# The last pair of experts in a two-layer transformer kernel: row products, gating and transposes in another order

## The chip, the cores and the metric

The kernel is one program on one NeuronCore of a Trainium2 chip. The metric is the device time of one launch in microseconds (us); of several runs the median is taken. The engines named here are TensorE (PE in the profile, its weight loads PEld), VectorE (DVE), ScalarE (ACT), GpSimd (POOL) and SyncE (SP), which in this kernel issues the loads from HBM. All data are 32-bit floats, and each matmul in the source leaves two records in the trace, so that "x16" in a row of PE is eight matmuls of the program (transposes written as such leave one record each).

## The reference, cut to what matters

Two networks of two layers each run one after the other on 256 tokens of width 1024. In the second network each layer ends with a mixture of 32 experts, of which each token uses two. The change touches this part alone:

```
def expert_block(args):
    xblk, e = args
    hid = jax.nn.silu(xblk @ w_gate[e]) * (xblk @ w_up[e])
    return hid @ w_down[e]

yb = lax.map(expert_block, (xb, block_e)).reshape(n_rows, d)
return jnp.zeros_like(h).at[row_tok].add(yb * row_w[:, None])
```

A router picks the experts and the weights `row_w`; `xb` holds the tokens' rows sorted by expert. An expert has 1024x512 gate and up weights and 512x1024 down weights. The weights of two experts are 12 MB, and all 16 pairs of a layer are read whatever the router says.

## The kernel before

`experts(l)` exists once for each engine and runs twice, for layer 0 (from about 824 us of the span) and layer 1 (from about 1385 us, up to the final norm). Each pair of experts i = 0..15 is worked on by hand-written code that is the same in shape for each i; each engine runs its own list in program order and waits on counters (semaphores) that the others raise.

**A pair on TensorE.** At most 64 tokens (`CAP`) go to an expert; two experts fill 128 rows of a product. `product_of(0, i, ...)` multiplies the gathered tokens `xg` with the gate weights into bank 0 of PSUM, `product_of(1, ...)` with the up weights into bank 1: eight steps k, each of two matmuls of 64 columns of tokens against 512 weights (`gate_step`, the rows of L1543), the two experts side by side in the array. Steps 0 to 3 use the first half of a weight matrix, 4 to 7 the second; `half_arrived` waits for its load. `turn_hidden` transposes the gated rows `hs` (128x512) in four 128x128 pieces back into bank 0 (L1642); `turn_weights` transposes the router's weights for the pair (L1630, bank 2); `scatter` adds the rows of the pair before, `yt`, to the tokens' sums in banks 4 to 7, in eight products m = 0..7 (`add_rows`, L1504), of which m = 0..3 read the first half of `yt` and m = 4..7 the second. I call one of these eight a row product. `down` multiplies the transposed hidden rows `hg` with the down weights, columns 0..511 (c = 0) into bank 0 and then 512..1023 (c = 1) into bank 1, k = 0..3 in each (L1673).

**A pair on the other engines.** ACT turns bank 0 into its sigmoid (`gate_sig`) and, after `down`, copies banks 0 and 1 into the halves of `yt` (`yt_ready`, twice a pair). DVE multiplies sigmoid and gate (L3375 in the last pair), multiplies with bank 1 into `hs` once up is full (L3378, raises `hid_ready`), copies the transposed rows to `hg` (L3380, raises `hg_ready`), and copies the transposed weights to `spread` (L3383, raises `spread_ready`).

**The loads.** SP issues the weights of pair i as their places in SBUF come free, that is, as PE finishes with what lay there. For the last pairs they come in halves of 2 MB, and the second half of the last pair's down weights in two parts of 1 MB (`load_last_half`, L1836).

**The last pair** (i = 15) is written out by itself. Its row products stand: three between the halves of gate (`first_rows`), three between the halves of up (`later_rows`), one after up, one after `turn_weights`. Before the first up product PE waits for `yt_ready` to reach twice the pair's number.

**The start of the stage.** `keep_clock(n)` multiplies zeros with zeros into unused banks, n products of 128x128 (L1444). It is called twice in `experts`: between the two products that count the chosen experts, and after these, once the token rows are there (`htok_ready`), ahead of `gather(e_, 0)`. `gather` picks the first pair's tokens by a product with the mask `pick` (L1497), which DVE makes at L3284 (`masks_ready`).

Of the kernel before, what the change touches and what calls it, by code (L numbers as in the profile page):

```python
# [17 lines left out]
ALU = mybir.AluOpType  # L18
# [3 lines left out]
P = 128  # L22
D = 1024
KT = D // P
# [11 lines left out]
HTL = HALF // P  # L36
# [24 lines left out]
EH = 512  # L61
# [104 lines left out]
def build(nc, a, out):  # L166
    with ExitStack() as ctx:
# [82 lines left out]
        ident = cst("ident")  # L250
# [361 lines left out]
        def _(pe):  # L612
# [810 lines left out]
            def experts(l):  # L1423
# [18 lines left out]
                def keep_clock(n):  # L1442
                    for i in range(n):
                        mm(ps[:, 4 + i % 4, 0:P], zeros[:, 0:P], zeros[:, 0:P], start=True, stop=True)  # L1444
# [17 lines left out]
                    open_bank(b)  # L1462
                    owner[b] = None
                turn.take(S["htok_ready"], 4)
                keep_clock(2)
                pe.wait_ge(e_["masks_ready"], 1)
                gather(e_, 0)
                gather(e_, 1)
# [131 lines left out]
            def gathered_tokens(e_, first):  # L1600
# [32 lines left out]
                def scatter(m0=0, m1=KT, begins=False):  # L1633
                    for m in range(m0, m1):
                        last = add_rows(m, begins=begins)
                    if m1 == KT:
                        last.then_inc(e_["scattered"], 1)

                def turn_hidden(i):
                    pe.wait_ge(e_["hid_ready"], i + 1)  # L1640
                    for m in range(HTL):
                        last = nc.tensor.transpose(ps[:, 0, m * P:(m + 1) * P], hs[:, m * P:(m + 1) * P], ident)  # L1642
                    last.then_inc(e_["hid_turned"], 1)
# [11 lines left out]
                        add_rows(m, of_first=True)  # L1655

                def down(i):
                    pe.wait_ge(e_["hg_ready"], i + 1)
                    for c in range(2):
                        in_two = c == 1 and isinstance(i, int) and i == last_pair  # L1660
                        if in_two:
                            first_part_arrived(first)
                        else:
                            half_arrived(first, 2, i, c)
                        for k in range(HTL):
                            if in_two and k == HTL // 2:
                                half_arrived(first, 2, i, c)
                            for e in range(2):
                                at = k * PAIR + e * CAP
                                tile, to = tile_of(first, 2, i, c, e, k), ps[e * CAP:(e + 1) * CAP, c, :]  # L1670
                                if places_of(2, i)[c] is None:
                                    to = to.rearrange("p (a b) -> p a b", a=4)
                                last = mm(to, hg[:, at:at + CAP], tile, start=(k == 0), stop=(k == HTL - 1))  # L1673
                        last.then_inc(e_["down_done" if c else "half_done"], 1)
# [38 lines left out]
                    scatter(0, 3)  # L1713

                def later_rows():
                    scatter(3, KT - 2)

                product_of(0, last_pair, 0, e_["gate_full"], first_rows)
                pe.wait_ge(e_["yt_ready"], 2 * last_pair)
                product_of(1, last_pair, 0, e_["up_full"], later_rows)  # L1720
                scatter(KT - 2, KT - 1)
                turn_hidden(last_pair)
                turn_weights(last_pair)
                scatter(KT - 1, KT)
                down(last_pair)

# [752 lines left out]
        def _(dve):  # L2479
# [851 lines left out]
            def gathered_tokens(e_):  # L3331

                def hidden_rows(i):
                    dve.wait_ge(e_["gate_sig"], i + 1)
                    V.tensor_tensor(eg, ps[:, 0, :], sg, ALU.mult).then_inc(e_["gated"], 1)  # L3335
                    dve.wait_ge(e_["gated"], i + 1)
                    dve.wait_ge(e_["up_full"], i + 1)
                    V.tensor_tensor(hs, ps[:, 1, :], eg, ALU.mult).then_inc(e_["hid_ready"], 1)  # L3338
                    dve.wait_ge(e_["weights_turned"], i + 1)

                def turned(i):
                    V.tensor_copy(spread, ps[:, 2, 0:T]).then_inc(e_["spread_ready"], 1)
                    dve.wait_ge(e_["hid_turned"], i + 1)
                    V.tensor_copy(hg, ps[:, 0, :]).then_inc(e_["hg_ready"], 1)

                last_pair = NEXP // 2 - 1
                for i in range(2):
                    dve.wait_ge(e_["gate_sig"], i + 1)
                    V.tensor_tensor(eg, ps[:, 0, :], sg, ALU.mult).then_inc(e_["gated"], 1)
                    dve.wait_ge(e_["weights_turned"], i + 1)  # L3350
                    V.tensor_copy(spread if i else first_spread, ps[:, 2, 0:T]).then_inc(e_["spread_ready"], 1)
                    masks(e_, i + 1)
                    dve.wait_ge(e_["gated"], i + 1)
                    dve.wait_ge(e_["up_full"], i + 1)
                    V.tensor_tensor(hs, ps[:, 1, :], eg, ALU.mult).then_inc(e_["hid_ready"], 1)
                    dve.wait_ge(e_["hid_turned"], i + 1)
                    V.tensor_copy(hg, ps[:, 0, :]).then_inc(e_["hg_ready"], 1)
                def middle_pair(i):
                    hidden_rows(i)
                    masks(e_, i + 1)  # L3360
                    if isinstance(i, int) and i < BLOCKS:
                        dve.wait_ge(e_["scattered"], i - 1)
                        turned(i)
                    else:
                        dve.wait_ge(e_["hid_turned"], i + 1)
                        V.tensor_copy(hg, ps[:, 0, :]).then_inc(e_["hg_ready"], 1)
                        dve.wait_ge(e_["scattered"], i - 1)
                        V.tensor_copy(spread, ps[:, 2, 0:T]).then_inc(e_["spread_ready"], 1)

                for i in range(2, BLOCKS + 1):  # L3370
                    middle_pair(i)
                with dve.Fori(0, last_pair - BLOCKS - 1) as n:
                    middle_pair(n + BLOCKS + 1)
                dve.wait_ge(e_["gate_sig"], last_pair + 1)
                V.tensor_tensor(eg, ps[:, 0, :], sg, ALU.mult).then_inc(e_["gated"], 1)  # L3375
                dve.wait_ge(e_["gated"], last_pair + 1)
                dve.wait_ge(e_["up_full"], last_pair + 1)
                V.tensor_tensor(hs, ps[:, 1, :], eg, ALU.mult).then_inc(e_["hid_ready"], 1)  # L3378
                dve.wait_ge(e_["hid_turned"], last_pair + 1)
                V.tensor_copy(hg, ps[:, 0, :]).then_inc(e_["hg_ready"], 1)  # L3380
                dve.wait_ge(e_["scattered"], last_pair - 1)
                dve.wait_ge(e_["weights_turned"], last_pair + 1)
                V.tensor_copy(spread, ps[:, 2, 0:T]).then_inc(e_["spread_ready"], 1)  # L3383
# [272 lines left out]
```

## Time and profile before

| | |
|---|---|
| median of 3 runs | 1843.9 us (1843.64 to 1845.76) |
| the profiled execution: its device time | 1845.65 us |
| its span, first to last instruction | 1843.8 us |
| TensorE busy | 1787.9 us, 97% of the span |
| VectorE, ScalarE busy | 781.4 us, 387.5 us |
| loads on the hardware queue | 589.63 MB |
| chain that ended last, by engine | PE 82%, DMA 14%, DVE 2%, ACT 1% |
| mean granted TensorE clock | 0.992 |

The times of the profile count from the span's start. A row of the timeline says when an instruction started, how long it took, its engine and line, output and input by name, and in brackets how long the engine had been idle before it and what ended that. Work that overlaps on one engine is pipelined: a matmul's record lasts longer than the time after which the next can start.

### The profile page before, as it was taken

What the parts mean: (1) busy time and instruction counts of PE and PEld (TensorE: products, weight loads), DVE (VectorE), ACT (ScalarE), POOL (GpSimd) and SP (SyncE); (2) the same over time, 40 slices, a digit from 0 to 9 for tenths busy, and PEclk for the clock granted to TensorE, in tenths of its full rate; (3) what the DMA queues carried; (4) which work ended last, traced back from release to release, by engine and by line L of the source; (5) the groups of instructions that cost most, each with busy time, mean ns of one, the idle gap of its engine ahead of it and who ended that gap; (6) DMA issues with size and microseconds to landing.
All of it is one profiled execution on the core that took longest, in us unless ns stands there. A gap on an engine that the chain in (4) does not pass through costs nothing.

```text
span 1843.8 us, 25756 instructions
## 1 busy us (share of the span) xinstructions
PE 1787.9 (97%) x10782; PEld 1197.4 (65%) x10786; DVE 781.4 (42%) x1501; ACT 387.5 (21%) x830; POOL 17.8 (1%) x31
## 2 busy tenths in 40 slices
PE   8999999999999999999999998899999999998998
PEld 7799999858999997674454343345985444443333
DVE  5978878873886964533111011014533111110112
ACT  3441110433311113522211111112113211110111
POOL 1000000000000100000000000000000000000000
PEclk9999999999999999999999999999999999999999
DMA  8664687725347764159999999999478999999996
GB/s 313 228 274 163 270 336 303 292 101 221 145 191 290 312 241 191 71 211 358 427 427 433 425 433 428 433 424 425 200 279 342 427 427 429 430 431 431 430 427 254
DMA packets 55406, 593.31 MB, mean 322 GB/s; under 512 B 6272, under 2 KB 18560, under 8 KB 22400
## 3 DMA queue, kind: packets, MB, share of 16 engines
q1 hardware_dynamic: 54720, 589.63, 77.7%
q10 hardware_dynamic: 576, 2.10, 0.3%
q8 instruction: 84, 1.38, 0.3%
q14 instruction: 26, 0.21, 0.0%
HBM read 588.91 MB, written 1.05 MB: 320 GB/s over the span
## 4 chain that ended last, share of the span: by engine, by line
PE 82%; DMA 14%; DVE 2%; ACT 1%; issue 1%; DVEq 0%; SPq 0%
PE ps L1543 19%; PE ps L883 14%; DMA ring<-in_w_up 13%; PE ps L670 13%; PE ps L1673 8%; PE ps L960 8%; PE ps L1504 4%; PE ps L1497 2%; PE ps L745 1%; PE ps L824 1%; PE ps L1079 1%; PE ps L1321 1%; PE ps L1281 1%; PE ps L1738 1%; PE ps L730 1%; PE ps L777 1%
## 5 line engine op out<-in xcount | busy, mean ns | idle before, releaser
L1543 PE MATMUL ps<-ring,work 128*64 128x512 f32 x1376 | 312.6, 609 | 29.8 <-DMA ring<-in_w_up 29.8
L1543 PEld LDWEIGHTS ps<-ring,work 128*64 128x64 f32 x1376 | 100.5, 140 | 232.7 <-issue 198.9
L2020 ACT ACTIVATE work<-ps 128x512 f32<-128x512 f32 (+1 forms) x168 | 89.8, 539 | 702.9 <-PE ps L1673 248.5
L1673 PE MATMUL ps<-ring,work 128*64 128x512 f32 x896 | 199.0, 595 | 0.3
L3335 DVE TENSOR_TENSOR work<-ps,work 128x512 f32<-128x512 f32 x26 | 18.0, 692 | 382.8 <-ACT work L2020 382.8
L670 PE MATMUL ps<-hsq,ring 128*128 128x256 f32 x768 | 169.9, 380 | 0.3 <-DVE hsq L2575 0.3
L670 PEld LDWEIGHTS ps<-hsq,ring 128*128 128x128 f32 x768 | 144.7, 190 | 22.8 <-issue 3.4
L1543 PE MATMUL ps<-spare,work 128*64 128x512 f32 x528 | 148.6, 592 | 0.0
L883 PE MATMUL ps<-hsq,ring 128*128 128x128 f32 x1280 | 147.2, 275 | 0.6 <-issue 0.5
L883 PEld LDWEIGHTS ps<-hsq,ring 128*128 128x128 f32 x1280 | 145.2, 192 | 1.9 <-issue 1.7
L1673 PEld LDWEIGHTS ps<-ring,work 128*64 128x64 f32 x896 | 62.0, 137 | 120.8 <-issue 119.1
L1504 PE MATMUL ps<-work 128*128 128x256 f32 x512 | 121.5, 381 | 0.0
L883 PE MATMUL ps<-hsq,spare 128*128 128x128 f32 x960 | 110.5, 275 | 0.0
L883 PEld LDWEIGHTS ps<-hsq,spare 128*128 128x128 f32 x960 | 109.0, 192 | 0.4
L1543 PEld LDWEIGHTS ps<-spare,work 128*64 128x64 f32 x528 | 47.1, 137 | 95.5 <-issue 95.5
L2496 DVE SCALAR_TENSOR_TENSOR work<-ring,silu_c,work 128x512 f32<-128x512 f32 x140 | 105.2, 752 | 4.8
L1504 PEld LDWEIGHTS ps<-work 128*128 128x128 f32 x512 | 92.6, 190 | 18.2 <-issue 8.1
L3338 DVE TENSOR_TENSOR work<-ps,work 128x512 f32<-128x512 f32 x26 | 18.0, 692 | 194.2 <-PE ps L1543 194.2
L2020 ACT ACTIVATE work<-hsq 128x512 f32 x60 | 38.1, 635 | 208.7 <-PE ps L1543 201.7
L670 PE MATMUL ps<-work,ring 128*128 128x256 f32 x352 | 79.1, 382 | 0.9 <-DVE work L3175 0.9
L670 PEld LDWEIGHTS ps<-work,ring 128*128 128x128 f32 x352 | 66.1, 190 | 13.8 <-issue 3.9
L1543 PE MATMUL ps<-work 128*64 128x512 f32 x144 | 64.8, 593 | 0.0
(386 smaller groups left out, 2019.1 us busy)
## 6 DMA issues: line engine op xcount, KB each, us to landing
ring<-in_w_up SPq DMA_DIRECT2D x30, 2048.0 KB, 13.3
ring<-in_w_up SPq DMA_DIRECT2D x14, 4096.0 KB, 21.7
ring<-in_w_down SPq DMA_DIRECT2D x14, 4096.0 KB, 20.5
ring<-in_w_ada SPq DMA_DIRECT2D x24, 2048.0 KB, 13.6
ring<-in_w_gate SPq DMA_DIRECT2D x24, 2048.0 KB, 12.9
ring<-in_w_down SPq DMA_DIRECT2D x24, 2048.0 KB, 16.3
spare<-in_w_gate SPq DMA_DIRECT2D x10, 3072.0 KB, 19.2
ring<-in_w_ff_gate SPq DMA_DIRECT2D x10, 2048.0 KB, 8.4
```

Of the source, the lines that this page charges most:

```text
L670: last = mm(ps[:, b, 0:T], w[:, k, m * P:(m + 1) * P], rhs[:, k, :], start=(i == 0), stop=(i == nk - 1))
L730: last = mm(ps[:, b, 0:P], w[:, k, m * P:(m + 1) * P], rhs[:, k, half(t)], start=(k == 0), stop=(k == KT - 1))
L745: last = mm(ps[:, banks[m], half(t)], w[:, k, m * P:(m + 1) * P], u[:, k, half(t)], start=(k == 0), stop=(k == KT - 1))
L777: last = mm(ps[QUAD * g:QUAD * g + QUAD, b, 0:T], taps_of(GROUPS * j + g), data_of(GROUPS * j + g), start=start, stop=stop)
L883: last = mm(ps[:, b, at:at + P], tile_of(w, k, m), rows[:, k, :], start=(begins and w == m == k == 0), stop=(k == HTL - 1), skip_group_che ...
L960: last = mm(ps[:, b, m * P:(m + 1) * P], tile_of(k, m), rows[:, k, :], start=(s == m == k == 0), stop=(k == nk - 1), skip_group_check=True)
L1497: last = mm(ps[:, 3 - half, k * PAIR:(k + 1) * PAIR], htok[:, t, (4 * half + k) * P:(4 * half + k + 1) * P], pick[:, t, :], start=(t == 0) ...
L1504: return mm(ps[:, 4 + m // 2, (m % 2) * T:(m % 2 + 1) * T], rows, first_spread if of_first else spread, start=begins and m % 2 == 0, stop= ...
L1543: last = mm(ps[e * CAP:(e + 1) * CAP, w, :], xg[:, k, e * CAP:(e + 1) * CAP], tile_of(first, w, i, 2 * k // KT, e, k % HTL), start=(k == 0 ...
L1673: last = mm(to, hg[:, at:at + CAP], tile, start=(k == 0), stop=(k == HTL - 1))
L2020: return nc.scalar.activation(out_, in_, f, bias=bias, scale=scale, **kw)
L2496: return V.scalar_tensor_tensor(out=out_, in0=in0, scalar=scalar, in1=in1, op0=op0, op1=op1)
```

## The change

Four things change, in both layers:

1. The second call of `keep_clock(2)` goes.
2. Row products 3 and 4 move from between the halves of up to ahead of up (behind the wait for `yt_ready`); row product 5 stays between the halves.
3. DVE makes `hs` in two instructions of 256 columns, each raising `hid_ready`. PE transposes columns 0..255 into bank 0, the weights next, then columns 256..511 into bank 3 (`turn_half`); DVE copies the two parts to `hg` by two instructions of 256 columns, each raising `hg_ready`.
4. `down` of the last pair begins once the first part of `hg` is there and waits for the second ahead of k = 2.

```
                 turn.take(S["htok_ready"], 4)
-                keep_clock(2)
                 pe.wait_ge(e_["masks_ready"], 1)
...
                 def down(i):
+                    of_last = isinstance(i, int) and i == last_pair
                     pe.wait_ge(e_["hg_ready"], i + 1)
...
                         for k in range(HTL):
+                            if of_last and c == 0 and k == HTL // 2:
+                                pe.wait_ge(e_["hg_ready"], last_pair + 2)
...
                 def later_rows():
-                    scatter(3, KT - 2)
+                    scatter(KT - 3, KT - 2)
+
+                def turn_half(part):
+                    pe.wait_ge(e_["hid_ready"], last_pair + 1 + part)
+                    for m in range(HTL // 2 * part, HTL // 2 * (part + 1)):
+                        last = nc.tensor.transpose(ps[:, 3 * part, m * P:(m + 1) * P], hs[:, m * P:(m + 1) * P], ident)
+                    last.then_inc(e_["hid_turned"], 1)
...
                 pe.wait_ge(e_["yt_ready"], 2 * last_pair)
+                scatter(3, KT - 3)
                 product_of(1, last_pair, 0, e_["up_full"], later_rows)
                 scatter(KT - 2, KT - 1)
-                turn_hidden(last_pair)
+                turn_half(0)
                 turn_weights(last_pair)
+                turn_half(1)
                 scatter(KT - 1, KT)
                 down(last_pair)
...
-                V.tensor_tensor(hs, ps[:, 1, :], eg, ALU.mult).then_inc(e_["hid_ready"], 1)
-                dve.wait_ge(e_["hid_turned"], last_pair + 1)
-                V.tensor_copy(hg, ps[:, 0, :]).then_inc(e_["hg_ready"], 1)
+                parts = [slice(p * EH // 2, (p + 1) * EH // 2) for p in range(2)]
+                for cols in parts:
+                    V.tensor_tensor(hs[:, cols], ps[:, 1, cols], eg[:, cols], ALU.mult).then_inc(e_["hid_ready"], 1)
+                for p, cols in enumerate(parts):
+                    dve.wait_ge(e_["hid_turned"], last_pair + 1 + p)
+                    V.tensor_copy(hg[:, cols], ps[:, 3 * p, cols]).then_inc(e_["hg_ready"], 1)
```

On TensorE, from the first up product of layer 1's last pair to the start of down, the program before has these rows (L1543 up, L1504 row products, L1642 and L1630 transposes, L1673 down; in brackets the counters waited for):

```order
L1543 MATMUL ps<-ring,work 64x512 [waits slot5_loaded,expert_yt_ready_1]
L1543 MATMUL ps<-ring,work 64x512 x7
L1504 MATMUL ps<-work 128x256 x3
L1543 MATMUL ps<-ring,work 64x512 [waits slot6_loaded]
L1543 MATMUL ps<-ring,work 64x512 x7
L1504 MATMUL ps<-work 128x256
L1642 MATMUL ps<-con,work 128x128 [waits expert_hid_ready_1]
L1642 MATMUL ps<-con,work 128x128 x3
L1630 MATMUL ps<-con,work 128x128 [waits expert_spread_ready_1,expert_masks_ready_1]
L1630 MATMUL ps<-con,work 128x128
L1504 MATMUL ps<-work 128x256
L1673 MATMUL ps<-ring,work 64x512 [waits slot0_loaded,expert_hg_ready_1]
```

The changed program has at the head of this stretch (its lines are numbered differently: L1542 up, L1503 row products):

```order
L1503 MATMUL ps<-work 128x256 [waits expert_yt_ready_1]
L1503 MATMUL ps<-work 128x256
L1542 MATMUL ps<-ring,work 64x512 [waits slot5_loaded]
L1542 MATMUL ps<-ring,work 64x512 x7
L1503 MATMUL ps<-work 128x256
L1542 MATMUL ps<-ring,work 64x512 [waits slot6_loaded]
```

Two row products stand ahead of up and one between its halves. At the end of the stretch, from the row product after up on, it has (L1723 transposes of the hidden rows, L1629 of the weights, L1675 down):

```order
L1503 MATMUL ps<-work 128x256
L1723 MATMUL ps<-con,work 128x128 [waits expert_hid_ready_1]
L1723 MATMUL ps<-con,work 128x128
L1629 MATMUL ps<-con,work 128x128 [waits expert_spread_ready_1,expert_masks_ready_1]
L1629 MATMUL ps<-con,work 128x128
L1723 MATMUL ps<-con,work 128x128 [waits expert_hid_ready_1]
L1723 MATMUL ps<-con,work 128x128
L1503 MATMUL ps<-work 128x256
L1675 MATMUL ps<-ring,work 64x512 [waits slot0_loaded,expert_hg_ready_1]
L1675 MATMUL ps<-ring,work 64x512 x3
L1675 MATMUL ps<-ring,work 64x512 [waits expert_hg_ready_1]
L1675 MATMUL ps<-ring,work 64x512 x3
```

The weights' transposes now stand between the two halves of the hidden rows' transposes, and down has one wait more.

On VectorE the last pair of layer 1 stands in the program before as:

```order
L3375 TENSOR_TENSOR work<-ps,work 128x512 [waits expert_gate_sig_1]
L3378 TENSOR_TENSOR work<-ps,work 128x512 [waits expert_up_full_1,expert_gated_1]
L3380 COPY work<-ps 128x512 [waits expert_hid_turned_1]
L3383 COPY work<-ps 128x256 [waits expert_weights_turned_1,expert_scattered_1]
L3402 UNCONDITIONAL_BRANCH
```

and in the changed one as:

```order
L3385 TENSOR_TENSOR work<-ps,work 128x512 [waits expert_gate_sig_1]
L3390 TENSOR_TENSOR work<-ps,work 128x256 [waits expert_up_full_1,expert_gated_1]
L3390 TENSOR_TENSOR work<-ps,work 128x256
L3393 COPY work<-ps 128x256 [waits expert_hid_turned_1] x2
L3396 COPY work<-ps 128x256 [waits expert_weights_turned_1,expert_scattered_1]
```

Two instructions of 512 columns have become four of 256.

## Rows read from the trace of the kernel before

**Rows 1.** The chain that ended last (start us, us, what), last two pairs.

```profile
1756.64 8.78 PE ps L1543 x32
...
1787.04 23.58 DMA ring<-in_w_up
```

**Rows 2.** Timeline, TensorE and VectorE, layer 1's last pair from the second half of gate.

```profile
1806.57 0.64 PE L1543 MATMUL ps<-spare,work 128*64 128x512 f32 x1
...
1810.76 3.65 PE L1543 MATMUL ps<-ring,work 128*64 128x512 f32 x16 [0.53 <-DMA ring<-in_w_up]
...
1814.35 1.56 PE L1504 MATMUL ps<-work 128*128 128x256 f32 x6
...
1815.84 3.65 PE L1543 MATMUL ps<-ring,work 128*64 128x512 f32 x16
...
1819.61 0.69 DVE L3378 TENSOR_TENSOR work<-ps,work 128x512 f32<-128x512 f32 x1 [8.01 <-PE ps L1543]
...
1820.36 0.66 PE L1642 MATMUL ps<-con,work 128*128 128x128 f32 x4 [0.23 <-DVE work L3378]
...
1821.05 0.69 DVE L3380 COPY work<-ps 128x512 f32<-128x512 f32 x1 [0.75 <-PE ps L1642]
1821.07 0.60 PE L1504 MATMUL ps<-work 128*128 128x256 f32 x2
1821.70 0.42 DVE L3383 COPY work<-ps 128x256 f32<-128x256 f32 x1
...
1821.80 7.09 PE L1673 MATMUL ps<-ring,work 128*64 128x512 f32 x32
```

**Rows 3.** Issues on SP for this pair's up weights, and the second one's time to landing.

```profile
1787.04 3.76 SPq L1815 DMA_DIRECT2D ring<-in_w_up  x2
...
ring<-in_w_up SPq DMA_DIRECT2D x1, 2048.0 KB, 25.0
```

**Rows 4.** The same for its down weights: three issues, their times to landing.

```profile
1798.33 0.33 SPq L1815 DMA_DIRECT2D ring<-in_w_down  x1
1801.76 0.90 SPq L1836 DMA_DIRECT2D ring<-in_w_down  x2
...
DMA to landing us min/median/max: 21.2/22.1/23.2
```

**Rows 5.** Timeline around the first gather, layer 1, then layer 0.

```profile
1390.72 0.43 DVE L3284 TENSOR_TENSOR work<-con,work 128x256 f32<-128x256 f32 x1
1391.09 0.69 PE L1444 MATMUL ps<-zeros 128*128 128x128 f32 x4
1391.62 3.74 PE L1497 MATMUL ps<-work 128*128 128x128 f32 x32
1393.60 1.51 ACT L2020 ACTIVATE work<-ps,ada,scale_g 128x128 f32<-128x128 f32 x4 [1.94 <-PE ps L1497]
...
829.63 0.42 DVE L3284 TENSOR_TENSOR work<-con,work 128x256 f32<-128x256 f32 x1
830.52 3.74 PE L1497 MATMUL ps<-work 128*128 128x128 f32 x32
```

**Rows 6.** Stretch: engines' busy time (instructions), granted clock, DMA share, GB/s; SP's issue.

```profile
1424.00:1426.00 2.00, 2.00 (x12) 0.61 (x10) 0.00 (x0) 0.00 (x0) 0.00 (x0) 1.00 0.81 229
...
1424.45 0.33 SPq L1810 DMA_DIRECT2D spare<-in_w_up  x1
```

**Rows 7.** Timeline from layer 0's last pair to the first products of layer 1's mixer.

```profile
1257.24 3.65 PE L1543 MATMUL ps<-ring,work 128*64 128x512 f32 x16
...
1281.64 1.23 DVE L2732 TENSOR_TENSOR spare<-ring 128x1024 f32<-128x1024 f32 x1 [1.27 <-DMA ring<-in_w_odd]
...
1285.03 3.31 ACT L2020 ACTIVATE hsq<-hsq,ada 128x256 f32<-128x256 f32 x8 [3.20 <-DVE hsq L3433]
...
1288.76 3.73 PE L883 MATMUL ps<-hsq,ring 128*128 128x128 f32 x32 [0.50 <-issue]
```

**Rows 8.** A stretch after a long wait of TensorE; columns as in Rows 6.

```profile
1756.00:1764.00 8.00, 7.36 (x28) 2.36 (x30) 0.00 (x0) 0.00 (x0) 0.00 (x0) 0.79 0.95 410
```

More of the change, by code:

```diff
@@ L1657, in down @@
                 def down(i):
+                    of_last = isinstance(i, int) and i == last_pair
                     pe.wait_ge(e_["hg_ready"], i + 1)
                     for c in range(2):
-                        in_two = c == 1 and isinstance(i, int) and i == last_pair
+                        in_two = c == 1 and of_last
                         if in_two:
```

## Prediction

> **What bounds the kernel now.** I read the chain that ended last first, then the timeline of each place that the diff names, and last the issues and landings of the loads there. In the last pairs of a layer the chain alternates between TensorE products and the loads of the up weights: 8.78 us of products in pair 13, and then, for pair 15, a load of up weights that ran 23.58 us from its issue at 1787.04 [rows 1]. It landed at 1810.62, and TensorE began the up products at 1810.76, 0.14 us later, after 0.53 us without work [rows 2]. From there to the end nothing is late but TensorE itself and the two hand-overs with VectorE between up and down: up's second half began at 1815.84, the gated rows were made from 1819.61 to 1820.30, turned from 1820.36, copied from 1821.05 to 1821.74, and down began at 1821.80 [rows 2]. That is 5.96 us from the start of up's second half to down. Down's own loads were not late: issued at 1798.33, 1801.76 and about 1802.2, with 22.1, 21.2 and 23.2 us to landing, they were there at 1820.4, 1823.0 and 1825.4 [rows 4].
>
> **Steps of TensorE that I use.** The 16 records of a half of gate or up take 3.59 us until a row product can start (1810.76 to 1814.35), and six records, three row products, take 1.49 us until the products of 64 columns go on (1814.35 to 1815.84) [rows 2]. At 0.43 us each, the rate at which eight pairs of side by side records fill 3.43 us of a half, three are 1.30 and the change back costs 0.19; the change into them costs 0.15. So one row product costs 0.43, and a group of them 0.34 more wherever it stands between such products.
>
> **Part 1, the zeros ahead of the first gather.** The zeros began at 1391.09 and the gather at 1391.62. What the gather needs besides is the mask, finished by VectorE at 1390.72 + 0.43 = 1391.15 [rows 5]. VectorE's hand-over to TensorE took 0.06 us at the turns [rows 2]; I allow up to 0.14, the delay seen behind a load. So the gather begins between 1391.21 and 1391.29, that is 0.33 to 0.41 us earlier; I take 0.35. ScalarE waited 1.94 us for the gather's first half and had nothing else to do, so it moves along [rows 5]. In layer 0 the mask ended at 830.05 and the gather began at 830.52, the same distance: 0.35 again. Does this reach the end, when later pairs wait for loads? The stream of loads is full only from a certain point on; in the stretch from 1424 the DMA share was still 0.81 with 229 GB/s, and the next issue, at 1424.45, waited for a product of TensorE [rows 6]. Everything behind that gap is issued and lands earlier by as much as TensorE is. So both the products and the stream shift by 0.35 in each layer.
>
> **Part 2, two row products ahead of up.** The second half of gate began at 1806.57 and would end, for a row product, at 1810.16. Two row products and the change back take 0.87 + 0.19 = 1.06: up can begin at 1811.21, 0.45 later than before. The load landed at 1810.62, so nothing is waited for. Up's first half, one row product and the change back take 3.59 + 0.43 + 0.19 = 4.21 (before 5.08), so TensorE would be ready for the second half at 1815.42, 0.42 earlier than 1815.84: the wait and its reaction (0.77 over the pure sequence) are filled, less 0.34 for one more group of row products. But now the second load counts. Its issue is the last 0.33 us of a row of two that ends at 1790.80, thus 1790.47, and it took 25.0 us: landed at 1815.47 [rows 3]. With the reaction of 0.14 the second half begins at 1815.61. The gain is 0.23 and not 0.42.
>
> **Part 3, hidden rows in two parts.** Counting from the start of up's second half: VectorE begins at +3.77. A PSUM instruction of 512 columns took 0.69 as product or as copy, a copy of 256 took 0.42 [rows 2]; no row here shows the product at 256, and between 0.35 (half of 0.69) and 0.42 I take the copy's 0.42, since product and copy agree at 512. First part ready +4.19, turned from +4.25. Six transposes fill the 0.71 us from 1820.36 to the row product at 1821.07, so one occupies TensorE for 0.12; the copy of four began 0.69 after their start, 0.22 behind the last one's slot [rows 2]. Two then take 0.24 and are seen at 0.46: the first copy runs from +4.71 to +5.13 and down could start at +5.19. TensorE meanwhile: weights' transposes to +4.73, the second half's to +4.97 (its rows were ready at about +4.6), the last row product with the change back 0.62, to +5.59. Down starts at +5.59, held by TensorE's own work, against +5.96: 0.37 gained, between 0.2 (if the second hand-over costs TensorE another 0.15) and 0.45. The second copy of `hg` ends near +5.6 and is needed at +5.59 + 1.72. At 1815.61 + 5.59 = 1821.20 the down weights of 1820.4 are there; the last of them, 1825.4, is wanted at 1826.4.
>
> The Trainium skill speaks against this part: VectorE: DVE Perf Modes, section on the TRN2 errata, says that each VectorE instruction pays a fixed latency and advises tiles of 512 elements or more. The trace agrees about the price: 0.69 and 0.42 leave a fixed part of 0.15, twice more here. By that rule alone the part would lose 0.30; it doesn't, as the second parts lie beside TensorE's row product.
>
> **Layer 0's last pair** would gain in the same way, and I book nothing for it. Its up half began at 1257.24; the pair ends some 13 us before the next mixer. There VectorE waited for a load of the odd layer's weights until 1281.64, with 1.27 us idle; behind that stand the reciprocal and the eight scalings, which feed ScalarE until 1288.34; and TensorE, idle for 0.50 us, began at 1288.76 [rows 7]. That load is in the full stream, which moves with part 1 and not with the last pair. What TensorE gains in the last pair it waits longer at 1288.76.
>
> **The sum.** 0.35 + 0.35 from the gathers, 0.23 + 0.37 from layer 1's last pair: 1.3 us. Against the profiled execution's 1845.65 (its span 1843.8 and 1.85 around it) that is 1844.35. This execution lies at the upper end of the three runs; on their median, 1843.9, it gives 1842.6, and that is the forecast.
>
> **Rivals.**
> (a) Layer 0's last pair counts after all, by 0.5 us: if TensorE and not ScalarE ends the 0.50 us of idle time at 1288.76. Against it stands that ScalarE's eighth row ends at 1288.34, later than the last product before. It would give 1842.1.
> (b) The stream of loads does not follow the gather, because its rate and not the gap of rows 6 decides when the late loads land. Then part 1 is swallowed in both layers, and 0.6 is left: 1843.3.
> (c) The last pair gives nothing: the load of up's second half lands a little later against TensorE than here, or the second hand-over in three steps costs what the first saves. Parts 2 and 3 cancel and part 1 stays: 1843.2.
> (d) Slower: the zeros kept TensorE's clock. After a wait of some 4 us the granted clock was 0.79 in a stretch of 8 us, partly at the lower level of 1.2 GHz [rows 8], and the up products took 8.78 us, where the 32 records of down took 7.09 at full clock: 1.7 us lost [rows 1, 2]. If each gather fell so, the loss is 3.4 against gains of 1.3: 2.1 slower, 1846.0. It decides once the two layers together lose 1.3 us, which is 2.6 us at half rate. A loss over 0.2% would need about 10 us at half rate. Against it: the zeros fill only 0.45 us and the mask's wait leaves at most 0.2 us idle in their place; the other call stays.
> The Trainium skill, TensorE: Matmul & The Clock Gate, Part 1, says that the gate goes by how busy the array has lately been; that is the ground of (d), and the stretch of rows 8, behind a wait, agrees.
> That the change doesn't do what it says is (c) in another form.
>
> **How the numbers follow.** A measurement of this kernel can tell about 0.2%, 3.7 us, from no change. Forecast 0.55, (a) 0.12, (b) 0.13, (c) 0.15, (d) 0.05. All but the far end of (d) lie within 0.2%. What can lead beyond is the spread of the runs: before's three span 2.1 us, so a median may lie 1.9 above or somewhat below. I give faster 0.03, within 0.95, slower 0.02. The range: the cases' own times reach from 1842.1 to 1843.3; 1 us below for terms that are larger than worked out, and the 1.9 us above for a median at the upper end of the runs, give 1841.1 to 1845.2.
>
> **What would show it.** The gather should follow the counts with 0.1 to 0.2 us between, and begin near 0.35 us earlier after the mask. In layer 1's last pair the first up product should have no wait, the second half should begin right behind a landing, 4.4 after the first; down should begin 5.6 after up's second half, with two row products ahead of up. The idle time at the line of 1288.76 should grow from 0.50 to near 1.0. Wrong it would be if the granted clock dips at the gather, if down waits for a load, or if that idle time stays.

## The result, and the profile after

The changed kernel is slower: 1851.45 us, median of 6 runs (1851.05 to 1853.3), against 1843.85 (1843.44 to 1846.41) of 6 runs of the kernel before on the same chip. The ratio is 1.004, with a 95% interval of 1.0029 to 1.0051, so 5.3 to 9.4 us are lost. The prediction was 1842.6, in a range of 1841.1 to 1845.2, with 2 in 100 for slower.

The two profiles compared are of an execution of 1845.65 us (before, span 1843.8) and one of 1851.05 (after, span 1849.3): 5.5 us apart in span. That is less than the 7.6 between the medians because before's is 1.8 above its median and after's 0.4 below its own.

The page of after, engines (busy us, share of the span, instructions) and the queue q8, which I take below for the one that brings TensorE's program code:

```profile
span 1849.3 us, 25748 instructions
...
PE 1790.8 (97%) x10778; PEld 1197.5 (65%) x10778; DVE 781.1 (42%) x1505; ACT 386.9 (21%) x830; POOL 17.7 (1%) x31
...
q8 instruction: 85, 1.39, 0.3%
```

TensorE is busy for 2.9 us more than before, with fewer products. The timeline of after in layer 1, from the mask on, shows where (start, duration, engine, line, output and input, and in brackets the idle time before and what ended it). It answers to rows 5, and its lines L3294 and L1496 are the mask and the gather there, L1542 the gate and up products:

```profile
1389.62 0.42 DVE L3294 TENSOR_TENSOR work<-con,work 128x256 f32<-128x256 f32 x1
...
1390.19 3.81 PE L1496 MATMUL ps<-work 128*128 128x128 f32 x32
...
1393.93 7.08 PE L1542 MATMUL ps<-ring,work 128*64 128x512 f32 x30
...
1395.90 2.08 SPq L1832 DMA_DIRECT2D ring<-in_w_down  x2
...
1405.56 1.87 PE L1542 MATMUL ps<-ring,work 128*64 128x512 f32 x2 [4.55 <-issue]
...
1407.35 0.69 PE L1629 MATMUL ps<-con,work 128*128 128x128 f32 x2
...
1407.97 8.26 PE L1542 MATMUL ps<-ring,work 128*64 128x512 f32 x32
...
1416.16 2.05 PE L1496 MATMUL ps<-work 128*128 128x128 f32 x16
```

The reader should see the x30. The gate products of pair 0 are 32 records; after 30 of them TensorE stops for 4.55 us, in the middle of step k = 7. Nothing is released there: "issue" means that the profile shows no wait for data. The weights of k = 7 are there, since they came with those of k = 4 to 6. What follows is slow too: two records take 1.87 us and the 32 of up 8.26, where down's 32 take 7.09. The same stretch in windows of 2 us (busy time and instructions of the engines, granted clock, DMA share, GB/s):

```profile
1400.00:1402.00 2.00, 1.01 (x4) 0.12 (x1) 0.00 (x0) 0.00 (x0) 0.00 (x0) 1.00 1.02 307
1402.00:1404.00 2.00, 0.00 (x0) 0.00 (x0) 0.00 (x0) 0.00 (x0) 0.00 (x0) 0.89 0.65 256
1404.00:1406.00 2.00, 0.44 (x1) 0.18 (x1) 0.00 (x0) 0.00 (x0) 0.00 (x0) 0.50 0.06 23
1406.00:1408.00 2.00, 2.00 (x6) 0.32 (x4) 0.00 (x0) 0.50 (x1) 0.00 (x0) 0.50 0.03 8
1408.00:1410.00 2.00, 2.00 (x7) 0.74 (x8) 0.57 (x1) 1.38 (x2) 0.00 (x0) 0.50 0.86 254
```

TensorE stands still from about 1401; the granted clock falls to 0.50, the level of 1.2 GHz, while it stands, and stays there until 1410 (from 1410 to 1411 it is 0.82, then 1.00). The kernel before has, in this place, the products in one piece:

```profile
1395.28 7.09 PE L1543 MATMUL ps<-ring,work 128*64 128x512 f32 x32
1402.67 7.09 PE L1543 MATMUL ps<-ring,work 128*64 128x512 f32 x32
1409.69 2.05 PE L1497 MATMUL ps<-work 128*128 128x128 f32 x16
```

**The account of the 5.5 us**, by the start of rows in both timelines. Up to layer 1's first gather after is 1.43 ahead (1390.19 against 1391.62). From this gather to the next one it takes 25.97 us (to 1416.16) against 18.07 (to 1409.69): 7.90 lost. From there to the last up half it is 406.16 against 406.15: nothing. Up's second half to down, 5.49 against 5.96: 0.47 won. From down to the end of the span 21.49 against 22.00: 0.51 won, in four products of the final norm that the change doesn't touch. They took 1.22 us before, at a granted clock of 0.50, and 0.71 after, at 1.00:

```profile
1836.21 1.22 PE L1763 MATMUL ps<-con,small 128*128 128x128 f32 x4 [0.62 <-DVE small L3482]
```

The sum: 7.90 - 1.43 - 0.47 - 0.51 + 0.01 = 5.5. One place loses more than all the rest wins.

The last pair of layer 1 in after, which answers to rows 2, shows the intended effects (L1503 row products, L3390 the gated rows, L1723 their transposes, L3393 the copies, L1675 down):

```profile
1816.34 1.13 PE L1503 MATMUL ps<-work 128*128 128x256 f32 x4
...
1817.43 3.65 PE L1542 MATMUL ps<-ring,work 128*64 128x512 f32 x16
...
1821.02 0.70 PE L1503 MATMUL ps<-work 128*128 128x256 f32 x2
...
1822.32 3.65 PE L1542 MATMUL ps<-ring,work 128*64 128x512 f32 x16 [0.61 <-DMA ring<-in_w_up]
...
1826.09 0.76 DVE L3390 TENSOR_TENSOR work<-ps,work 128x256 f32<-128x256 f32 x2 [8.32 <-PE ps L1542]
...
1826.58 0.44 PE L1723 MATMUL ps<-con,work 128*128 128x128 f32 x2
...
1827.05 0.86 DVE L3393 COPY work<-ps 128x256 f32<-128x256 f32 x2 [0.20 <-PE ps L1723]
...
1827.81 7.09 PE L1675 MATMUL ps<-ring,work 128*64 128x512 f32 x32
```

And layer 0's (rows 7), where the clock falls at the gather as well, and the seam with the mixer:

```profile
829.24 0.42 DVE L3294 TENSOR_TENSOR work<-con,work 128x256 f32<-128x256 f32 x1
829.81 5.44 PE L1496 MATMUL ps<-work 128*128 128x128 f32 x32
...
1280.55 1.23 DVE L2742 TENSOR_TENSOR spare<-ring 128x1024 f32<-128x1024 f32 x1 [2.04 <-DMA ring<-in_w_odd]
...
1287.44 0.38 PE L897 MATMUL ps<-marks 128*128 128x512 bf16 x1 [1.04 <-issue]
```

### The profile page after: what moved, and what is told of

It reads as the page before. It is cut to its first block, busy times and chain, and to the rows that moved or that the text cites. A ratio compares the mean times of both kernels' runs of the same rounds, so it can differ in the third digit from the quotient of the medians.

```text
span 1849.3 us, 25748 instructions
## 1 busy us (share of the span) xinstructions
PE 1790.8 (97%) x10778; PEld 1197.5 (65%) x10778; DVE 781.1 (42%) x1505; ACT 386.9 (21%) x830; POOL 17.7 (1%) x31
## 4 chain that ended last, share of the span: by engine, by line
PE 80%; DMA 16%; DVE 2%; issue 1%; ACT 1%; DVEq 0%; SPq 0%
PE ps L1542 18%; DMA ring<-in_w_up 16%; PE ps L883 14%; PE ps L670 13%; PE ps L1675 8%; PE ps L960 7%; PE ps L1503 3%; PE ps L1496 2%; PE ps L745 1%; PE ps L824 1%; PE ps L1079 1%; PE ps L763 1%; PE ps L1321 1%; PE ps L1281 1%; PE ps L1748 1%
## 5 line engine op out<-in xcount | busy, mean ns | idle before, releaser
L1542 PE MATMUL ps<-ring,work 128*64 128x512 f32 x1376 | 313.5, 608 | 33.5 <-DMA ring<-in_w_up 29.0
L1542 PEld LDWEIGHTS ps<-ring,work 128*64 128x64 f32 x1376 | 99.3, 140 | 237.0 <-issue 198.1
L1675 PE MATMUL ps<-ring,work 128*64 128x512 f32 x896 | 199.0, 595 | 0.0
L1542 PE MATMUL ps<-spare,work 128*64 128x512 f32 x528 | 148.7, 593 | 0.0
L1675 PEld LDWEIGHTS ps<-ring,work 128*64 128x64 f32 x896 | 62.0, 137 | 120.4 <-issue 118.8
L1503 PE MATMUL ps<-work 128*128 128x256 f32 x512 | 122.0, 382 | 0.0
L1542 PEld LDWEIGHTS ps<-spare,work 128*64 128x64 f32 x528 | 47.4, 137 | 95.4 <-issue 95.1
L1503 PEld LDWEIGHTS ps<-work 128*128 128x128 f32 x512 | 92.4, 190 | 19.7 <-issue 9.7
L1542 PE MATMUL ps<-work 128*64 128x512 f32 x144 | 64.8, 593 | 0.0
```

The source lines that it names most:

```text
L1503: return mm(ps[:, 4 + m // 2, (m % 2) * T:(m % 2 + 1) * T], rows, first_spread if of_first else spread, start=begins and m % 2 == 0, stop= ...
L1542: last = mm(ps[e * CAP:(e + 1) * CAP, w, :], xg[:, k, e * CAP:(e + 1) * CAP], tile_of(first, w, i, 2 * k // KT, e, k % HTL), start=(k == 0 ...
```

## The experiments

**The theories.** Seven of pair 0's eight gate steps, 28 records, stand ahead of the branch `with pe.If(most > CAP)`; its `Else`, `gathered_tokens`, begins with k = 7. After stops 2 records behind the branch. Theory P: TensorE waits for its own program code. The code comes in blocks on the queue q8 (84 packets with 1.38 MB before, 16.4 KB each, which is 256 machine instructions of 64 bytes as they lie in the built program), and the changed kernel's `Else` happens to stand just ahead of a block's end; the cause is the place of the code, not the work that was taken out. Where the text on record says P1, it is the form of it in which the next block's fetch is held up by the weights' loads. The rivals: the zeros' removal itself (the clock, or the earlier gather; rival (d) of the prediction), or the new order of the last pair, does it.

I counted TensorE's machine instructions in the built programs, modulo 256. A float32 product is four of them (two weight loads, two matmuls), which is two records of the timeline; the first one behind the branch is no product but the mark of the branch's target. The `Else` of layer 1 begins at position 216 before and at 201 after: the zeros' removal moves it by 14, the rest by 1. The profile doesn't show where a block ends; 207 in this count is fitted to where after and before_pad60 (experiment 2) stopped, and experiments 3 and 4 test it. With it, 6 instructions are left in after's block: one, and a product of four, and one more weight load. That is 28 + 2 records, what the timeline shows. TensorE's own branch instruction begins at 1395.8 and lasts 3.92 us,

```profile
L1482 PEldq COMPARE_BRANCH  x1: 3920/3920/3920, 1395.8 to 1395.8; - x1
```

and the trace has two fetches behind it, in views of single stretches of 0.2 us: for after at 1396.8 to 1397.0 and at 1403.2 to 1403.4,

```profile
q8 instruction: 1, 0.02, 47.4%
...
q8 instruction: 1, 0.02, 29.6%
```

so work goes on 2.2 to 2.4 us behind the second. The kernel before fetches at nearly the same distance (1398.2 and 1404.4), but its `Else` stands 247 instructions ahead of a block's end, some 22 us of products, and nothing waits. Its next fetch comes at 1423.9, when these have about run out.

**1. The same code on another place: after_pad4.** The changed kernel with four products in the branch that is never taken, `all_tokens`, which stands ahead of `gathered_tokens`. What runs is not altered; the `Else` moves from 201 to 217.

```
             def all_tokens(e_, first):

+                if first == moe_first[1]:
+                    for i in range(4):
+                        mm(ps[:, 4, 0:P], zeros[:, 0:P], zeros[:, 0:P], start=True, stop=True)
```

> The changed kernel, with four products of zeros more at the head of the branch of layer 1 that is not taken (all_tokens). Nothing that runs is altered; the branch's target and all behind it stand 16 machine instructions of TensorE later in the program. Theory P (place of the code): the 4.55 us without work in the middle of layer 1's gate step k = 7 is a wait for the next block of TensorE's code behind the branch; it goes, with the slow products behind it, 7.8 us in all: 1843.6, and the row of that step has no idle time. Rival Z (the zeros' removal itself, by the clock or by what it shifts in time): the wait stays, 1851.4. Rival L (the last pair's new order costs the time): 1851.4.

Measured: 1843.98 us (1842.72 to 1846.3, 10 runs) against 1844.27 of before, ratio 0.9995 [0.9985, 1.0004]. The loss is gone. In the timeline the gate products are whole again, though the gather ran at the lower clock (5.44 instead of 3.81):

```profile
1391.04 5.44 PE L1496 MATMUL ps<-work 128*128 128x128 f32 x32
...
1396.40 7.09 PE L1542 MATMUL ps<-ring,work 128*64 128x512 f32 x32
...
1403.79 7.09 PE L1542 MATMUL ps<-ring,work 128*64 128x512 f32 x32
```

**2. The loss without the change: before_pad60.** The same edit with `range(60)` on the kernel before: 240 instructions, position 200, 7 left.

> The kernel before, with sixty products of zeros in the branch of layer 1 that is not taken, which puts the branch's target at the same place within a block of 256 instructions as in the changed kernel (position 200, there 201; before it was 216). Theory P: a wait of 4 to 5 us appears in layer 1's gate step k = 7 and the time is about 1851. Rivals Z and L: nothing that runs has changed, 1843.9.

Measured: 1853.54 us (1850.26 to 1854.45, 5 runs), ratio 1.004 [1.0027, 1.0054]. The kernel before, with all its zeros and its old last pair, stops in the same place, and one record later than after, as one more instruction in the block allows:

```profile
1394.97 7.08 PE L1543 MATMUL ps<-ring,work 128*64 128x512 f32 x31
...
1406.14 1.12 PE L1543 MATMUL ps<-ring,work 128*64 128x512 f32 x1 [4.09 <-issue]
...
1407.81 9.36 PE L1543 MATMUL ps<-ring,work 128*64 128x512 f32 x32
```

These two runs decide between the theories: no instruction that runs differs, and 7 to 9 us come and go.

**3. The parts by themselves: rows_and_halves, no_zeros, no_zeros_pad4.** The first is the changed kernel with `keep_clock(2)` back in its place (position 215); the second is before without it (position 202, 5 left); the third is the second with four products as in experiment 1 (218).

```
                 turn.take(S["htok_ready"], 4)
-                keep_clock(2)
```

> Parts 2 to 4 alone: the changed kernel with the zeros ahead of the first gather put back. The target of layer 1's branch stands at position 215. Theory P: no wait behind the branch; the last pair gives what its rows give, down 5.5 after up's second half (before 5.96): 1843.3 to 1843.6. Rival L: 1846 to 1851. Rival Z: 1843.4.

> Part 1 alone, with no padding: the zeros ahead of the first gather are gone and nothing else has changed. The target of layer 1's branch stands at position 202, 5 machine instructions ahead of the block's end. Theory P: the whole loss comes with this part alone, by the place of the code: a wait of 4 to 5 us in layer 1's gate step k = 7 after 29 or 30 records, time 1851 to 1852, where the same kernel with 16 machine instructions more in the branch not taken took 1844.8. Rival (parts 2 and 3 are needed for it): 1844.

> Part 1 alone, with four products of zeros in layer 1's branch not taken (target at position 218). Theory P: no wait behind the branch; what is left is the gather's start 0.4 us earlier and, if the zeros kept the clock, a gather at the lower level in layer 0 (5.4 us for 3.7): 1843.2 to 1845. Rival Z: about 1851 whatever the place of the code. Rival L: 1843.2.

Measured: rows_and_halves 1844.58 (11 runs), 1.0001 [0.9992, 1.001]; no_zeros 1852.42 (1850.09 to 1856.78, 5 runs) against 1844.77, 1.0046 [1.0031, 1.0061]; no_zeros_pad4 1844.77 (10 runs) against 1844.27, 1.0002 [0.9992, 1.0011]. So part 1 alone makes the whole loss, and only by where it leaves the code. The 1843.3 to 1843.6 that I expected of rows_and_halves, a gain of its own, didn't show. no_zeros:

```profile
1392.41 7.08 PE L1542 MATMUL ps<-ring,work 128*64 128x512 f32 x30
...
1404.50 1.97 PE L1542 MATMUL ps<-ring,work 128*64 128x512 f32 x2 [5.01 <-issue]
```

**4. More code left in the block: after_pad56.** Experiment 1 with 56 products: position 169, 38 left.

> The changed kernel with 56 products of zeros in layer 1's branch not taken: its target stands at position 169, and 38 machine instructions lie between it and the block's end at 207 (in the changed kernel 6, in before_pad60 7; both figures fit where their products stopped, after 30 and 31 records). Theory P (wait for the next block of code): TensorE gets 16 records further, 3.6 us of work, into the up product, before it runs out; a wait of about 1.0 us stands there instead of 4.55, the clock stays, and the time is 1845 to 1846. If a wait of 4 to 5 us stays in k = 7, or goes altogether, P is wrong in how it counts.

Measured: 1845.51 (10 runs) against 1845.36, 1.0005 [0.9996, 1.0015]. The wait came where 38 instructions end: one, 8 for the four records of k = 7, 4 for the two transposes of the weights, 24 for the first 12 records of up, 37 in all. I had expected 1.0 us and it was 1.68; the second block came later than I had worked out. The clock stayed at 1.00 behind it, and the loss doesn't show in the time (the profiled execution, 1849.36, is the slowest of the ten):

```profile
1403.22 2.80 PE L1542 MATMUL ps<-ring,work 128*64 128x512 f32 x12
...
1407.70 4.51 PE L1542 MATMUL ps<-ring,work 128*64 128x512 f32 x20 [1.68 <-issue]
```

**5. The loads out of the way: late_quarters.** The changed kernel, but SP holds back the 2 MB of down weights that it issues beside the gate products of layer 1, until these are over.

```
                         sp.wait_ge(*done(0, 0, 0, quarter))
+                        if l == 1:
+                            sp.wait_ge(e_["gate_full"], 1)
                         load_quarter(quarter)
```

> The changed kernel (target at position 201), in which SP in layer 1 issues the two quarter loads of pair 1's down weights only after the whole gate product of pair 0, so that no load is under way while TensorE fetches code. Theory P1 (the second block of code stands behind these 2 MB of loads in the DMA engines' rings): the second fetch starts 1 to 2 us after the first, the wait in k = 7 shrinks to under 1 us, the time falls by some 6 us, less what the later loads cost. Theory P2 (the second block is asked for a fixed 6 us after the first, whatever the loads do): the wait stays at 4.5 us and the time at 1851 or above.

Measured: 1849.03 (6 runs) against 1845.36, 1.0025 [1.0013, 1.0038]; the delayed loads are in this time. The wait went from 4.55 to 1.72 us, with no data on the DMA engines in two windows of the stretch:

```profile
1393.50 7.08 PE L1542 MATMUL ps<-ring,work 128*64 128x512 f32 x30
...
1402.30 1.02 PE L1542 MATMUL ps<-ring,work 128*64 128x512 f32 x2 [1.72 <-issue]
```

```profile
1397.00:1399.00 2.00, 2.00 (x12) 0.70 (x10) 0.00 (x0) 0.00 (x0) 0.00 (x0) 1.00 0.00 0
1400.00:1403.00 3.00, 1.28 (x4) 0.13 (x1) 0.00 (x0) 0.00 (x0) 0.00 (x0) 1.00 0.00 0
```

The two fetches stand at 1396.8 and 1399.9, 3.2 us apart, where after had 6.4. So the loads account for about half of the distance and most of the wait, but I had expected 1 to 2 us between the fetches, a wait of less than 1 us and a time some 6 us lower, and some 1.7 us of wait stay when the DMA engines are idle; what sets the 3.2 us between the fetches then is open. The clock stayed at 1.00 and the two records took 1.02 instead of 1.87, so the lower clock in after is a consequence of the longer wait.

**6. The same in layer 0: before_pad18_l0, before_pad12_l0.** The edit of experiment 2 for `moe_first[0]`, with 18 and with 12 products: positions 201 and 177 in layer 0 (before: 129). Layer 1's move to 32 and 8, far ahead of a block's end.

> The kernel before with 18 products of zeros in layer 0's branch not taken, which puts the target of layer 0's branch at position 201 (before 129) and that of layer 1 at 32 (before 216). Theory P: the wait of 4 to 5 us now stands in layer 0's gate step k = 7, none in layer 1; the time is 1850 to 1852, unless layer 0's slack behind swallows part. Rivals: nothing that runs has changed, 1843.9.

> The kernel before with 12 products of zeros in layer 0's branch not taken: target of layer 0's branch at position 177, of layer 1's at 8. With 18 products (201) layer 0 showed no wait, so either layer 0's blocks end some instructions earlier than 207, or layer 0 has no such wait. Theory P with an earlier end (195 to 201): TensorE runs out of code in layer 0 some 20 machine instructions behind the target, with 2 to 3.5 us without work there, and 1846 to 1849 in time. Theory that layer 0 is different (its code is fetched in time): no wait, 1844.

Measured: before_pad18_l0 1844.32 (10 runs) against 1845.36, 0.9993 [0.9983, 1.0002], with no wait anywhere; I had expected one, and it is a miss. before_pad12_l0 1848.61 (1846.51 to 1852.03, 10 runs) against 1844.77, 1.0019 [1.0009, 1.0028], with a wait in layer 0:

```profile
841.85 1.50 PE L1543 MATMUL ps<-ring,work 128*64 128x512 f32 x5
...
846.89 5.35 PE L1543 MATMUL ps<-ring,work 128*64 128x512 f32 x16 [3.53 <-issue]
```

Four records of k = 7, two transposes and 5 records of up take 1 + 8 + 4 + 10 = 23 instructions, and the next record's weight load comes only behind the wait: the block ends at 177 + 23 = 200. In layer 0 the block's end stands at 200 of my count and in layer 1 at 207. Then before_pad18_l0 put the `Else` just behind a block's end, the best place there is. The drift of 7 between the layers is in my count: the built program has one mark for each branch target, and seven of them stand between the two places. Left out of the count, they leave one end for all: after, before_pad60, no_zeros, after_pad56, late_quarters and before_pad12_l0 all stop at 194 modulo 256, with 5, 6, 4, 37, 5 and 22 instructions behind the target.

**7. The last pair's two parts apart: rows_only, halves_only.** One run each. rows_only is before with part 2 alone (`scatter(3, KT - 3)` ahead of up, `scatter(KT - 3, KT - 2)` between its halves), halves_only is before with parts 3 and 4 alone.

> Part 2 alone (two row products ahead of up), zeros and hidden rows as before; target of layer 1's branch at position 216. One look: in layer 1's last pair no wait ahead of up's first product or one under 0.2 us, up's second half held by its load and 4.9 us behind the first (before 5.08), up's second half to down 5.97 as before. Layer 0's idle time ahead of the next mixer 0.6 to 0.7.

> Part 3 and 4 alone (hidden rows in two parts), zeros and row products as before; target of layer 1's branch at position 217. One look: up's second half to down 5.5 us (before 5.96), first half of up to second 5.08 as before; layer 0's idle time ahead of the next mixer grows from 0.50 to about 0.9; no wait behind the branch.

Measured: 1845.5 beside 1844.77, and 1843.94 beside 1845.36; from one run each nothing follows for the time. In the timelines, from the start of up's first half to its second, and from there to down: before 5.08 and 5.96, rows_only 4.89 and 5.96, halves_only 5.08 and 5.49, rows_and_halves 4.90 and 5.48. rows_only's row of the second half and halves_only's of the gated rows, copies and down:

```profile
1810.90 3.65 PE L1543 MATMUL ps<-ring,work 128*64 128x512 f32 x16
...
1815.79 3.65 PE L1543 MATMUL ps<-ring,work 128*64 128x512 f32 x16 [0.61 <-DMA ring<-in_w_up]
```

```profile
1813.99 3.65 PE L1543 MATMUL ps<-ring,work 128*64 128x512 f32 x16
...
1817.76 0.76 DVE L3390 TENSOR_TENSOR work<-ps,work 128x256 f32<-128x256 f32 x2 [8.62 <-PE ps L1543]
...
1818.71 0.86 DVE L3393 COPY work<-ps 128x256 f32<-128x256 f32 x2 [0.20 <-PE ps L1724]
...
1819.48 2.80 PE L1676 MATMUL ps<-ring,work 128*64 128x512 f32 x12
```

The parts don't disturb each other, and neither makes the loss. One expectation missed: in rows_only layer 0's idle time ahead of the next mixer was 2.33 us and not 0.6 to 0.7. VectorE waited 3.09 us for the odd layer's load there, against 1.27 before.

## Why the prediction was wrong

**The step that failed** is part 1, and with it the sum: "What the gather needs besides is the mask". I counted removed instructions as time alone, and put what their place in memory costs at nothing. The gather did come earlier behind the mask, but removing them moved every later instruction in the program's memory, and the code behind a taken branch became an input with its own arrival, which the sum did not have. What the runs showed in its place is a wait for code of 4.55 us behind layer 1's branch, with slow products behind it, 7.90 us in all. The trace of before could have warned of it: two fetches 6.2 us apart behind the branch. How far the change moves the `Else` can be counted in the built programs; where a block ends took a run that stopped. The Trainium skill, Runtime: NRT & Kernel Launch, section "Instruction fetch mechanics", says that code is streamed in blocks of 256 instructions and that a taken branch breaks the sequential prefetch. The trace agrees: all six stops come at one place modulo 256, and 240 instructions more in before_pad60 act like 16 fewer. The section calls the crossing of a block's end "mostly hidden"; behind this branch it cost 7 to 9 us, and there the measurement decides.

**Part 1's own term** held. The gather begins 0.15 us behind the mask's end in both layers (829.66 to 829.81, 1390.04 to 1390.19), 0.47 before: 0.32 won, 0.35 predicted.

**Part 2** held in kind: up began with no wait (after, rows_only) or 0.17 us of it (rows_and_halves), and the second half was held by its load, with 0.61 idle in all three. The distance of the halves was 4.89 and not 4.40. I had put up's first product 0.59 behind its load's landing; but in rows_and_halves both halves began at a landing, and the landings lie 4.9 apart there, as they did before (1810.62 and 1815.47, 4.85) and as 2048 KB at the 429 GB/s of after's stretch from 1790 to 1800 would (4.89). There the part takes TensorE from 0.23 behind the second landing to right behind it, and no further. It isn't so in each execution: in the profiles of after_pad4 and late_quarters the second half waited for nothing and came 4.24 and 4.28 behind the first, the 4.21 of my pure sequence:

```profile
1817.52 3.65 PE L1542 MATMUL ps<-ring,work 128*64 128x512 f32 x16
```

From the start of gate's second half to down, for which I had 14.63, it took 15.23 before, 15.06 in after, 15.26 in rows_and_halves and 14.38 in after_pad4. So parts 2 and 3 give from nothing to 0.85 there, by when the loads land, and whether that reached the end can't be told from runs that differ by more.

**Part 3** was mis-sized on the good side: 5.48 to 5.49 where I had 5.59, against 5.96; the gain is 0.48, not 0.37. My ends for it were 0.2 to 0.45. The row for it is the product of 256 columns that I had no row for: two of them took 0.76 together, the second 0.34 behind the first's 0.42, less than the 0.84 that I took. The fixed part of 0.15, which I had worked out from 0.69 and 0.42, priced the two products at 0.15 more than one of 512; measured 0.07.

**Layer 0's last pair** gave nothing, as predicted: down came 5.49 behind up's second half there too, and the idle time at the mixer's first products grew from 0.50 to 1.04 (after), 0.95 (halves_only) and 1.25 (rows_and_halves), while VectorE's wait for the odd layer's load grew from 1.27 to 2.04 in after. Rival (a) is out. In no_zeros_pad4, whose last pair is the old one, the idle time is the old 0.50:

```profile
1287.96 2.28 PE L883 MATMUL ps<-hsq,ring 128*128 128x128 f32 x19 [0.50 <-issue]
```

**Rival (d)** had the right sign, and the wrong mechanism and size. Its mechanism exists: with the zeros none of 14 gathers in seven profiles fell to the lower clock (all 3.74 us), without them 4 of 12 in six profiles did, at 5.44 against 3.81, 1.63 us each, near the 1.7 that I gave. By chance alone such a split would come in 3 of 100. In after it was layer 0's gather:

```profile
830.00:832.00 2.00, 2.00 (x11) 2.00 (x11) 1.69 (x10) 0.18 (x1) 0.00 (x0) 0.53 1.24 347
```

But of the medians it moves none that can be seen: after_pad4, which has no zeros and one such gather in its profile, has a ratio of 0.9995. Whether later waits for loads take in what is lost there isn't shown; in that profile, the slowest of its ten executions, layer 1's gather to down took 431.97 us, against 430.18 before. My 1846.0 for this rival also lay outside the range that I gave.

**The forecast's 1.3 us** can't be confirmed. after_pad4 is the change without the accident of its place, and its interval, 0.9985 to 1.0004, holds 1.3 us (0.9993) and no gain (1) alike. Whether the stream of loads follows the gather (rival (b)) is settled for large shifts: in after the 7.90 us lost at the start of layer 1 are still there at the last up half, and in before_pad12_l0 layer 0's gather to down took 436.84 us where before took 432.68. For a shift of 0.35 it stays open: between layer 0's gather and VectorE's wait for the odd layer's load, the time differs by 2 us from one profile to the next (451.1 before, 449.2 rows_and_halves, 450.1 no_zeros_pad4, 450.7 after). No version here is measurably faster than before.

## What to carry to other kernels

Taking instructions out, or adding them, anywhere ahead of a branch moves the code behind it; before the cost of an edit is summed, count where the target of each taken branch comes to stand in its block of 256 instructions, and put it just behind a block's end, with padding in the branch that isn't taken. Where a block ends shows only in a run that stops there; marks of branch targets aren't to be counted. When a kernel with less work is slower, look for idle time marked "issue" in the middle of a run of equal products, and move the code without changing what runs: two such runs told here the place from the work. A gain below a microsecond that ends at a load is as large as the landing of that load allows, and no larger, and the landing differs from one execution to the next.

## What the runs showed of the hardware

- Behind a taken branch the block after the target's own was fetched 6.4 us after that one in after (5.2 in before_pad60, 6.8 in no_zeros) with 2 MB of weights being issued beside it, and 3.2 us after it with idle DMA engines (late_quarters); TensorE went on 2.2 to 2.4 us behind the second fetch. So TensorE's code and its data get in each other's way on the DMA engines.
- The wait by the instructions left in the target's block, layer 1: 5.01 us with 5, 4.55 with 6, 4.09 with 7, 1.68 with 38, none with 247; in layer 0 3.53 with 23, none with 71 (before). The mark of the target is counted in each. At the first three and in layer 0 the granted clock fell to 0.50 during or behind the wait, and at the first three a run lost 7 to 9 us in all, 1.5 to 2.3 times the wait; with 38 left it stayed at 1.00.
- A gather of 32 records behind short, thin products ran at the lower clock in 4 of 12 cases without 0.45 us of zeros ahead of it, and in none of 14 with them.
